# Layer 1 MLP of a two-layer diffusion backbone: places of a three-place weight ring, order of token sums at the seam, and the place of one transfer in POOL's queue

## The chip, the core and the metric

One core of one Trainium2 chip runs the whole program in one launch. Its engines are PE (TensorE, matmuls), DVE (VectorE), ACT (ScalarE), POOL (GpSimd) and SP (SyncE, which here only issues transfers). Each runs its own queue in order, and semaphores order them against each other. The metric is device microseconds of one execution.

## The reference

Two layers, each a token mixer and a squared-ReLU MLP, with D = 1024, 1024 latent tokens, 256 context tokens and a hidden width of 4096. Layer 0 mixes by a grouped Fourier transform, layer 1 by windowed attention; layer 1 updates the latent tokens alone. The part of the change is the MLP of layer 1:

```python
def _sq_relu_mlp(h, w1, w2):
    return jnp.square(jax.nn.relu(h @ w1)) @ w2
...
h_lat = h_lat + g2 * _sq_relu_mlp(_modulate(_rms_norm(h_lat, norm2_g[i]), sh2, sc2), mlp_w1[i], mlp_w2[i])
```

All is float32. Each product is made of three matmuls on rounded numbers: high times high, high times low, low times high. So each operand needs a rounded high half, which ACT writes, and a low half (the full number less the high one), which DVE or POOL writes.

## The kernel before

**The MLP of layer 1** is `strassen_tail` (from L1665). It takes the 4096 hidden rows in 16 pairs of 2 x 128. Pairs 0 and 1 (`PLAIN = 2`) compute the first product in the plain way, in four blocks for the hidden row block (1 or 2) and the token half. From pair 2 on both products go by Strassen's scheme with seven products, M1 to M7. The first-weight operands of a pair are items 0 to 6 (`W1_ORDER`), the token operands are B11, B21, B22 and the sums T1 to T4, which are made once, at the seam between pair 1 and pair 2, and then held.

**TensorE's order in a pair p** is M1, product 1 of pair p - 1, M5, product 2, M6, product 3, M2, product 4, M7, product 5, M3, product 6, M4, and then product 0 of pair p itself (`Z_ORDER`, `DEFERRED`, `pair` in the tensor block). Each is 12 matmuls of 128x128 by 128x512: M1 to M7 at L2763 to L2765, the second products in four groups of three at L2780 to L2782. Before group m of product i, TensorE waits until the result of group m of product i - 1 is read out of its bank (`read_out`): by DVE (`acc`, L2559) for m = 0, 1, 2, by ACT (`side_read`, L2247) for m = 3, which POOL then adds (`add`, L2082).

**The first weights' ring.** Item i of a pair lies in place i % 3 of `w1h` and `w1l`. For each item ACT rounds (`high1`, L2194) and POOL writes the low half (`low1`, L58 with `l_w1l`). `high1` waits for the product that last read the place: items 3 to 6 for M1, M5, M6, M2 of the same pair (`Z_ORDER[i - 3]`), items 0, 1, 2 for M4, M7, M3 of the pair before. In the queues of ACT and POOL, item 1 of the next pair comes first, then item 0, then item 2 (`HIGH1`). SP loads the full numbers into four slots (`load1`, `W1_SLOT`), each load behind the `low1` or the sum that last read the slot. Two items are sums that POOL makes in place (`sum1`, L2070).

ACT's queue of a pair (`pair` in the scalar block) is written out by hand, as are those of DVE and POOL. In it `high1(p, 6)` stands directly ahead of `relu(p, "B11")`. On DVE the order is `zsum(p, "B11")`, `acc(p - 1, 4, (0,))`, `square(p, "B11")`, `acc(p - 1, 4, (1, 2, 3))`. `square` reads what `relu` (L2223) wrote. M1 of a pair also waits for `relu` of B21 of the pair before, which ACT does behind M4.

**The seam.** The sums T1 to T4 are made on DVE in four operations each: `third_sum` (L2469), `first_sum` (L2475), `second_sum` (L2481), `fourth_sum` (L2487), each of which needs the one before. ACT rounds them (`high_t`, L2254), POOL writes the low half of T2, DVE those of T1, T3 and T4 (`low_t`). They are interleaved by hand with the work of pair 1. M5 of pair 2 needs T1 with its low half.

**The end of layer 0's MLP.** `layer_tail` also prepares sums of layer 1's weights in memory: per pair SP copies, and POOL issues two accumulating transfers (`add_sums`, L910, 512 KB each). The first weights' stands in the middle of `outputs`, the second weights' at its end. In the last pair the second is POOL's last instruction before all engines meet at the end of the block; then a block of one instruction clears the semaphores, and the attention's part begins. Layer 1's MLP waits for all these transfers before it loads its weights.

Of the kernel before, what the change touches and what calls it, by code (L numbers as in the profile page):

```python
# [562 lines left out]
def layer_tail(nc, sem, sb, banks, layer, wp, early, s_pw, w1, w2, mod, meanw, eps, ident, nh, nl, ht,  # L563
# [76 lines left out]
    with ExitStack() as ph:  # L640
# [124 lines left out]
        with nc.Block() as block:  # L765
# [94 lines left out]
            def _(pool):  # L860
# [51 lines left out]
                def outputs(p, more):  # L912
                    add(p, "M5")
                    low2(p, "S2")
                    add(p, "M3")
                    if more and C:
                        low1(p + 1, 0)
                    low2(p, "S3")
                    for prod in ROWS[2:]:
                        add(p, prod)  # L920
                        if C and not more:
                            if prod == "M2":
                                next_modulation()
                            for k in {"M6": (1,), "M7": (2, 3), "M4": (4,)}.get(prod, ()):
                                own_sum(k)
                        if prod == "M1":
                            for name in W_LATE[2:]:
                                low2(p, name)
                            if more:
                                low1(p + 1, 1 if C else 0)  # L930
                            if C:
                                add_sums(p, 0)
                    if more and not C:
                        low1(p + 1, 1)
                    if C:
                        add_sums(p, 1)
# [728 lines left out]
def strassen_tail(nc, sem, sb, banks, wp, early, s_pw, w1, w2, sums, s_sums, mod, meanw, eps, ident, nh, nl, nl_at, ht, park, out):  # L1665
# [31 lines left out]
    RELUS = ["B11", "B22", "B12", "B21"]  # L1697
    HIGH1 = [1, 0, 2, 3, 4, 5, 6]
    W1_SLOT = [0, 1, 0, 2, 1, 2, 3]
# [39 lines left out]
    with ExitStack() as ph:  # L1739
# [122 lines left out]
        def w1_parts(p, i):  # L1862
            if is_plain(p) and i == 3:
                return (x[:, 3].rearrange("p (k n) -> p k n", k=HK) for x in (ah, al))
            return w1h[:, i % 3], w1l[:, i % 3]

        def w1_at(p, i):
            if is_plain(p):
                return PRE + 4 * p + i + 1
            return p * 7 + (PRE + 4 * PLAIN - 7 * PLAIN + HIGH1.index(i) + 1)  # L1870

# [84 lines left out]
        with nc.Block() as block:  # L1956
            @block.sync
            def _(sp):
# [62 lines left out]
                load2(1, 6, (1, 2))  # L2021
                load1(2, 4, None, (2, 2))
                load2(2, 3, (1, 3))

                def pair(p, more):
# [11 lines left out]
                    if more:  # L2037
                        load1(p + 1, 4, None, (p + 1, 2))
                        load2(p + 1, 3, (p, 3))
# [13 lines left out]
            def _(pool):  # L2053
# [36 lines left out]
                def pair(p, more):  # L2090
# [10 lines left out]
                    if more:  # L2101
                        low1(p + 1, 1)
                    add(p - 1, 5)
                    low2(p, 1)
                    add(p - 1, 6)
                    low2(p, 2)
                    if more:
                        low1(p + 1, 0)
                        sum1(p + 1, 2)
                    add(p, 0)  # L2110
# [45 lines left out]
                low2(1, 1)  # L2156
                low1(2, 1)
                low1(2, 0)
                sum1(2, 2)
                low2(1, 2)  # L2160
                for j in range(HK):
# [13 lines left out]
            def _(act):  # L2175
                def high1(p, i):
# [10 lines left out]
                    elif i >= 3:  # L2187
                        act.wait_ge(s_z, z_at(p, Z_ORDER[i - 3]))
                    elif type(p) is int and p == PLAIN:
                        act.wait_ge(s_z, z_at(1, ("B12", "B12", "B21")[i]))  # L2190
                    else:
                        act.wait_ge(s_z, z_at(p - 1, Z_ORDER[(6, 4, 5)[i]]))
                    hi, _ = w1_parts(p, i)
# [62 lines left out]
                def pair(p, more):  # L2256
# [17 lines left out]
                    if more:  # L2274
                        high1(p + 1, 1)
                    relu(p, "B22")
# [10 lines left out]
                    if more:  # L2287
                        high1(p + 1, 0)
                    high(p, "T3")
                    side_read(p, 0)  # L2290
                    high(p, "T4")
                    high2(p, 3)
                    if more:
                        high1(p + 1, 2)
                    high(p, "T1")

# [84 lines left out]
                high2(1, 1)  # L2381
                relu(1, "B12")
                high1(2, 1)
                high1(2, 0)
                relu(1, "B22")
                high2(1, 2)
                for j in range(HK):
                    high_t("T2", j)
                high(1, "T2")
                high(1, "T3")  # L2390
                for j in range(HK):
                    high_t("T4", j)
                relu(1, "B21")
# [41 lines left out]
            def _(dve):  # L2435
# [227 lines left out]
                acc(0, 6)  # L2663

                low2(1, 0)
                sum2(1, 1)
                square(1, "B11")
                low(1, "B11")
                for one in (third_sum, first_sum):
                    for j in range(HK):  # L2670
                        one(j)
                square(1, "B12")
                for j in range(HK):
                    second_sum(j)
                square(1, "B22")
                diffs(1)
                low(1, "T2")
                for j in range(HK):
                    fourth_sum(j)
                low(1, "T3")  # L2680
                acc(1, 0, (0, 1))
                diff(1, "T4")
                acc(1, 0, (2, 3))
                pair(PLAIN, True)
# [20 lines left out]
            def _(pe):  # L2705
# [35 lines left out]
                def hidden(p, prod):  # L2741
# [16 lines left out]
                    for j in range(HK):  # L2758
                        (wh, wl), (th, tl) = (w1h[:, i % 3, j], w1l[:, i % 3, j]), tokens(name, j)
                        dst = z_ps[Z_BANK[prod]][:]  # L2760
# [1005 lines left out]
```

## Time and profile before

| | us |
|---|---|
| median of three runs (2436.36 to 2440.77) | 2439.2 |
| the profiled execution | 2440.93 |
| its span, first to last instruction | 2439.4 |

| engine | busy us | share of the span |
|---|---|---|
| PE, matmuls | 2262.4 | 93% |
| DVE | 1763.2 | 72% |
| POOL | 1173.2 | 48% |
| ACT | 1160.8 | 48% |

The mean granted TensorE clock is 0.975 of full speed. In a row of the timeline stand the start in us from the span's start, the duration, the engine, the line, what it writes and reads, and in brackets how long the engine was idle before it and which operation ended that. The idle time counts from the recorded end of the matmul before, which lies beyond the moment at which the next could have started. A busy engine is no bound by itself: what counts is which wait ends last before TensorE can go on.

### The profile page before, as it was taken

Reading aid. Unit: us, or ns where it says so; the run is one execution under the profiler, and the core shown is the slowest. Engines: PE = TensorE matmul, PEld = TensorE weight load, DVE = VectorE, ACT = ScalarE, POOL = GpSimd, SP = SyncE. Lnnn points to the kernel's source line nnn. Section 1 sums busy time; section 2 is a strip of 40 time slices with the busy share of each in tenths; the row PEclk is TensorE's granted clock in tenths of the full one; section 3 lists DMA queues with packets and bytes.
Section 4 is the critical chain, followed back from the end, with each engine's and each line's share of the span. In section 5 each row is a group of like instructions: output and inputs, shape, how many; then the busy total and the mean of one; then the engine's idle time right before and its main releaser. Section 6 shows DMA issues by size and latency. Waiting matters only on the chain. (4 is left out here: it accounts for less than half of the span.)

```text
span 2439.4 us, 38342 instructions
## 1 busy us (share of the span) xinstructions
PE 2262.4 (93%) x11430; PEld 1872.2 (77%) x11430; DVE 1763.2 (72%) x2843; ACT 1160.8 (48%) x2133; POOL 1173.2 (48%) x970
## 2 busy tenths in 40 slices
PE   5989979999999999999699799888998999999998
PEld 3768868888888888888587677776776777777777
DVE  4653787777777777777674688871689787878787
ACT  5553443333333333333443588883345554545454
POOL 0003623433333444333646477665546666666664
PEclk9999999999999999999799899999998999999999
DMA  7434213444443345444312211105111212121212
GB/s 267 177 131 174 65 52 104 122 127 120 113 128 103 112 123 132 114 114 131 122 49 104 88 31 38 33 24 198 48 43 48 73 56 73 56 73 56 73 56 87
DMA packets 106150, 234.23 MB, mean 96 GB/s; under 512 B 9424, under 2 KB 18000, under 8 KB 102736
## 3 DMA queue, kind: packets, MB, share of 16 engines
q1 hardware_dynamic: 94432, 209.57, 26.3%
q0 software_dynamic: 8704, 16.78, 4.2%
q10 hardware_dynamic: 2928, 6.82, 0.8%
q8 instruction: 43, 0.70, 0.1%
q14 instruction: 43, 0.35, 0.1%
HBM read 216.35 MB, written 50.33 MB: 109 GB/s over the span
## 5 line engine op out<-in xcount | busy, mean ns | idle before, releaser
L877 POOL TENSOR_TENSOR ht<-ht,l_side 128x512 f32<-128x512 f32 x112 | 150.3, 1342 | 508.9 <-ACT l_side L1002 504.7
L51 PE MATMUL l_z_ps<-nh,l_w1h 128*128 128x512 f32 (+1 forms) x816 | 292.8, 359 | 6.5 <-POOL l_w1l L58 3.4
L53 PE MATMUL l_z_ps<-nh,l_w1l 128*128 128x512 f32 (+1 forms) x816 | 291.8, 358 | 0.0
L52 PE MATMUL l_z_ps<-nl,l_w1h 128*128 128x512 f32 (+1 forms) x800 | 285.7, 357 | 0.0
L1306 DVE SCALAR_TENSOR_TENSOR ht<-l_yy_ps,mod,ht 128x512 f32<-128x512 f32 x336 | 233.8, 743 | 10.9 <-PE l_yy_ps L1622 9.9
L2082 POOL TENSOR_TENSOR ht<-ht,l_side 128x512 f32<-128x512 f32 x112 | 150.7, 1346 | 99.3 <-ACT l_side L2247 99.3
L58 POOL TENSOR_TENSOR l_w1l<-early,l_w1h 128x512 fp32r<-128x512 f32 x104 | 138.6, 1340 | 114.8 <-ACT l_w1h L2194 114.7
L3503 POOL TENSOR_TENSOR sc<-sc,den 128x640 f32<-128x640 f32 (+1 forms) x128 | 149.5, 1200 | 89.8 <-DVE den L3585 89.8
L58 POOL TENSOR_TENSOR l_w2l<-l_w2f,l_w2h 128x512 fp32r<-128x512 f32 x128 | 168.7, 1323 | 40.2 <-ACT l_w2h L2204 35.4
L2780 PE MATMUL l_yy_ps<-l_ah,l_w2h 128*128 128x512 f32 x448 | 178.5, 399 | 6.8 <-DVE ht L2559 6.7
L1620 PE MATMUL l_yy_ps<-l_ah,l_w2h 128*128 128x512 f32 x448 | 178.5, 398 | 6.1 <-DVE ht L1306 6.1
L51 PEld LDWEIGHTS l_z_ps<-nh,l_w1h 128*128 128x128 f32 x816 | 154.9, 190 | 30.4 <-issue 4.0
L2782 PE MATMUL l_yy_ps<-l_ah,l_w2l 128*128 128x512 f32 x448 | 176.3, 394 | 0.0
L1621 PE MATMUL l_yy_ps<-l_al,l_w2h 128*128 128x512 f32 x448 | 176.0, 393 | 0.0
L1622 PE MATMUL l_yy_ps<-l_ah,l_w2l 128*128 128x512 f32 x448 | 175.8, 392 | 0.0
L2781 PE MATMUL l_yy_ps<-l_al,l_w2h 128*128 128x512 f32 x448 | 175.2, 391 | 0.0
L53 PEld LDWEIGHTS l_z_ps<-nh,l_w1l 128*128 128x128 f32 x816 | 154.9, 190 | 22.6
L58 DVE TENSOR_TENSOR l_al<-l_slot,l_ah 128x512 fp32r<-128x512 f32 x144 | 122.7, 852 | 63.6 <-ACT l_ah L995 34.2
L52 PEld LDWEIGHTS l_z_ps<-nl,l_w1h 128*128 128x128 f32 x800 | 151.9, 190 | 21.8 <-issue 0.5
L1002 ACT ACTIVATE l_side<-l_yy_ps,mod 128x512 f32<-128x512 f32 x112 | 76.8, 686 | 183.1 <-PE l_yy_ps L1622 183.1
L58 DVE TENSOR_TENSOR l_w2l<-l_w2f,l_w2h 128x512 fp32r<-128x512 f32 x112 | 107.4, 959 | 54.0 <-ACT l_w2h L2204 42.9
L2559 DVE SCALAR_TENSOR_TENSOR ht<-l_yy_ps,mod,ht 128x512 f32<-128x512 f32 x192 | 136.7, 741 | 5.3 <-PE l_yy_ps L2782 5.3
(339 smaller groups left out, 6495.5 us busy)
## 6 DMA issues: line engine op xcount, KB each, us to landing
l_aw<-ada SPq DMA_DIRECT2D x128, 256.0 KB, 2.9
maw<-ada SPq DMA_DIRECT2D x24, 1024.0 KB, 5.1
l_w1f<-w SPq DMA_DIRECT2D x32, 512.0 KB, 3.6
l_w2f<-w SPq DMA_DIRECT2D x32, 512.0 KB, 4.2
sums<-w SPq DMA_DIRECT2D x32, 512.0 KB, 5.1
sums<-w POOLq DMA_DIRECT2D x32, 512.0 KB, 8.3
early<-w SPq DMA_DIRECT2D x50, 256.0 KB, 2.7
l_w2f<-w SPq DMA_DIRECT2D x48, 256.0 KB, 2.7
```

The lines of the kernel that those rows point to most:

```text
L51: pe.matmul(out, lh, rh, start=first, stop=False)
L52: pe.matmul(out, lh, rl, start=False, stop=False)
L53: return pe.matmul(out, ll, rh, start=False, stop=last)
L58: return eng.tensor_tensor(lo, full, f32(hi), ALU.subtract)
L1306: dve.scalar_tensor_tensor(out=h, in0=y_ps[m][:], scalar=mod[:, layer, G2, c, 0:1], in1=h, op0=ALU.mult, op1=ALU.add).then_inc(s_acc, 1)
L1620: pe.matmul(y_ps[m][:], wh, a_h, start=first, stop=False, skip_group_check=not first)
L1621: pe.matmul(y_ps[m][:], wh, a_l, start=False, stop=False, skip_group_check=not first)
L1622: pe.matmul(y_ps[m][:], wl, a_h, start=False, stop=True, skip_group_check=not first).then_inc(s_y, 1)
L2082: pool.tensor_tensor(h, h, side[k % 2][:], ALU.add).then_inc(s_add, 1)
L2780: pe.matmul(y_ps[m][:], wh, a_h, start=start, stop=False, skip_group_check=not start)
L2781: pe.matmul(y_ps[m][:], wh, a_l, start=False, stop=False, skip_group_check=not start)
L2782: pe.matmul(y_ps[m][:], wl, a_h, start=False, stop=True, skip_group_check=not start).then_inc(s_y, 1)
```

## The change

It does four things.

1. The ring's places come from a table, `W1_RING = [0, 1, 2, 0, 1, 2, 1]`, and `W1_AFTER = [3, 6, 5, 0, 1, 2, 4]` names for each item the product that last read its place (an index into `Z_ORDER`; of the pair before for items 0 to 2). So item 0 follows M2, item 1 M4, item 2 M3 of the pair before, and item 6 follows M7 of its own pair.
2. The items are made in the order 0 to 6 (`HIGH1` is gone): in the queues of ACT and POOL item 0 takes item 1's place and item 1 item 0's. `sum1(p + 1, 2)` and `high1(p + 1, 2)` move by a step each, and `load1(p + 1, 4)` waits for `low1(p + 1, 1)` too.
3. At the seam `third_sum` moves ahead of pair 1's work on DVE, `first_sum`, `second_sum` and `fourth_sum` each move ahead as well, and ACT's roundings of T2 and T4 go ahead of relus and roundings of pair 1.
4. In the last pair of layer 0 the second accumulating transfer is issued directly behind the first.

```diff
@@ outputs (POOL, layer_tail)
                             if C:
                                 add_sums(p, 0)
+                                if not more:
+                                    add_sums(p, 1)
                     if more and not C:
                         low1(p + 1, 1)
-                    if C:
+                    if C and more:
                         add_sums(p, 1)
@@ strassen_tail
-    HIGH1 = [1, 0, 2, 3, 4, 5, 6]
+    W1_RING = [0, 1, 2, 0, 1, 2, 1]
+    W1_AFTER = [3, 6, 5, 0, 1, 2, 4]
@@ w1_parts, w1_at, hidden
-            return w1h[:, i % 3], w1l[:, i % 3]
+            return w1h[:, W1_RING[i]], w1l[:, W1_RING[i]]
-            return p * 7 + (PRE + 4 * PLAIN - 7 * PLAIN + HIGH1.index(i) + 1)
+            return p * 7 + (PRE + 4 * PLAIN - 7 * PLAIN + i + 1)
@@ SP, also for pair 2 before the loop
-                        load1(p + 1, 4, None, (p + 1, 2))
+                        load1(p + 1, 4, (p + 1, 1), (p + 1, 2))
@@ POOL, pair (the same for pair 2 before the loop)
                     add(p - 1, 4)
                     if more:
-                        low1(p + 1, 1)
+                        low1(p + 1, 0)
                     add(p - 1, 5)
                     low2(p, 1)
+                    if more:
+                        sum1(p + 1, 2)
                     add(p - 1, 6)
                     low2(p, 2)
                     if more:
-                        low1(p + 1, 0)
-                        sum1(p + 1, 2)
+                        low1(p + 1, 1)
                     add(p, 0)
@@ ACT, high1
                     elif i >= 3:
-                        act.wait_ge(s_z, z_at(p, Z_ORDER[i - 3]))
+                        act.wait_ge(s_z, z_at(p, Z_ORDER[W1_AFTER[i]]))
...
-                        act.wait_ge(s_z, z_at(p - 1, Z_ORDER[(6, 4, 5)[i]]))
+                        act.wait_ge(s_z, z_at(p - 1, Z_ORDER[W1_AFTER[i]]))
@@ ACT, pair
                     relu(p, "B11")
                     side_read(p - 1, 4)
                     if more:
-                        high1(p + 1, 1)
+                        high1(p + 1, 0)
...
                     square_last(p)
                     if more:
-                        high1(p + 1, 0)
+                        high1(p + 1, 1)
                     high(p, "T3")
                     side_read(p, 0)
                     high(p, "T4")
                     high2(p, 3)
+                    high(p, "T1")
                     if more:
                         high1(p + 1, 2)
-                    high(p, "T1")
@@ ACT, the seam
                 relu(1, "B12")
+                high1(2, 0)
                 high1(2, 1)
-                high1(2, 0)
+                for j in range(HK):
+                    high_t("T2", j)
                 relu(1, "B22")
                 high2(1, 2)
                 for j in range(HK):
-                    high_t("T2", j)
+                    high_t("T4", j)
                 high(1, "T2")
                 high(1, "T3")
-                for j in range(HK):
-                    high_t("T4", j)
                 relu(1, "B21")
@@ DVE, the seam
+                for j in range(HK):
+                    third_sum(j)
                 low2(1, 0)
                 sum2(1, 1)
                 square(1, "B11")
                 low(1, "B11")
-                for one in (third_sum, first_sum):
+                for one in (first_sum, second_sum):
                     for j in range(HK):
                         one(j)
                 square(1, "B12")
                 for j in range(HK):
-                    second_sum(j)
+                    fourth_sum(j)
                 square(1, "B22")
                 diffs(1)
                 low(1, "T2")
-                for j in range(HK):
-                    fourth_sum(j)
                 low(1, "T3")
-                acc(1, 0, (0, 1))
                 diff(1, "T4")
-                acc(1, 0, (2, 3))
+                acc(1, 0)
```

## Rows read from the trace of the kernel before

**Rows 1.** Waits of TensorE from 1780 us on: waiter, awaited, us, times, longest.
```profile
PE l_z_ps L2763 <- POOL l_w1l L58: 19.2, 13, 2.7
```

**Rows 2.** Timeline: M1 of pairs 4 and 5, and ACT ahead of the latter.
```profile
1924.82 0.49 PE L2763 MATMUL l_z_ps<-nh,l_w1h 128*128 128x512 f32 x1 [1.38 <-POOL l_w1l L58]
1961.85 0.59 ACT L2223 ACTIVATE l_slot<-l_z_ps 128x512 f32<-128x512 f32 x1
1963.01 0.61 ACT L2194 ACTIVATE l_w1h<-early 128x512 fp32r<-128x512 f32 x1
1965.11 0.49 PE L2763 MATMUL l_z_ps<-nh,l_w1h 128*128 128x512 f32 x1 [1.37 <-POOL l_w1l L58]
```

**Rows 3.** Timeline around M7 of pair 4, and two roundings in a row at the seam.
```profile
1816.35 1.14 ACT L2194 ACTIVATE l_w1h<-early 128x512 fp32r<-128x512 f32 x2
...
1945.28 0.60 ACT L2223 ACTIVATE l_slot<-l_z_ps 128x512 f32<-128x512 f32 x1 [0.20 <-DVE l_z_ps L2518]
1945.91 0.70 DVE L2525 SCALAR_TENSOR_TENSOR l_z_ps<-l_z_ps,l_slot 128x512 f32<-128x512 f32 x1
1946.52 1.40 DVE L2559 SCALAR_TENSOR_TENSOR ht<-l_yy_ps,l_gneg,ht 128x512 f32<-128x512 f32 x2
1949.76 0.39 PE L2780 MATMUL l_yy_ps<-l_ah,l_w2h 128*128 128x512 f32 x1
1949.96 0.63 ACT L2194 ACTIVATE l_w1h<-early 128x512 fp32r<-128x512 f32 x1 [2.05 <-PE l_z_ps L2765]
```

**Rows 4.** Timeline: a read-out on DVE and the group that waited for it.
```profile
1791.81 2.05 DVE L2559 SCALAR_TENSOR_TENSOR ht<-l_yy_ps,l_gneg,ht 128x512 f32<-128x512 f32 x3
1792.60 0.50 PE L2780 MATMUL l_yy_ps<-l_ah,l_w2h 128*128 128x512 f32 x1 [1.29 <-DVE ht L2559]
```

**Rows 5.** Holes and clock: timeline rows, and stretches (A:B, us, busy, granted PEclk, DMA).
```profile
48.08 0.50 PE L51 MATMUL seq_ps<-tabh,gh 128*128 128x512 f32 x1 [1.73 <-ACT uvf L289]
48.00:51.00 3.00, 2.92 (x13) 2.38 (x14) 2.30 (x4) 2.48 (x6) 0.00 (x0) 1.00 0.87 350
1762.83 0.50 PE L51 MATMUL l_z_ps<-nh,l_ah 128*128 128x512 f32 x1 [2.00 <-POOL l_al L58]
1763.00:1766.00 3.00, 3.00 (x9) 2.33 (x10) 2.84 (x4) 0.94 (x2) 0.00 (x0) 0.56 0.30 87
1883.08 0.79 PE L2763 MATMUL l_z_ps<-nh,l_w1h 128*128 128x512 f32 x1 [2.67 <-POOL l_w1l L58]
1887.39 0.40 PE L2780 MATMUL l_yy_ps<-l_ah,l_w2h 128*128 128x512 f32 x1
```

**Rows 6.** Timeline of the seam: DVE, ACT, and M1 and M5 of pair 2.
```profile
1812.92 3.79 DVE L2469 SCALAR_TENSOR_TENSOR l_t3f<-l_nf,l_dsh,l_t3f 128x512 f32<-128x512 f32 x4
1819.64 6.29 DVE L2481 SCALAR_TENSOR_TENSOR l_t2f<-l_t3f,mod,l_t2f 128x512 f32<-128x512 f32 x4
1834.60 0.58 ACT L2223 ACTIVATE l_slot<-l_z_ps 128x512 f32<-128x512 f32 x1
1835.32 0.76 PE L2763 MATMUL l_z_ps<-nh,l_w1h 128*128 128x512 f32 x1 [5.63 <-ACT l_slot L2223]
1839.61 5.87 DVE L58 TENSOR_TENSOR nl<-l_nf,nh 128x512 fp32r<-128x512 f32 x4
1845.63 0.77 PE L2763 MATMUL l_z_ps<-nh,l_w1h 128*128 128x512 f32 x1 [3.09 <-DVE nl L58]
```

**Rows 7.** Line L2469: duration ns min/median/max, starts, forms.
```profile
L2469 DVE SCALAR_TENSOR_TENSOR l_t3f<-l_nf,l_dsh,l_t3f x4: 739/742/1798, 1812.9 to 1816.0; 128x512 f32<-128x512 f32 x4
```

**Rows 8.** Layer 0's end: the last two transfers' issues, and the drains (ns, start).
```profile
1176.14 1.05 POOL L910 DMA_DIRECT2D sums<-w  x1
...
1186.88 1.17 POOL L910 DMA_DIRECT2D sums<-w  x1
L765 POOLq DRAIN  x1: 8092/8092/8092, 1184.7 to 1184.7; - x1
L765 DVEq DRAIN  x1: 1554/1554/1554, 1186.0 to 1186.0; - x1
```

More of the change, by code:

```diff
@@ L2021, in _ @@
                 load2(1, 6, (1, 2))
-                load1(2, 4, None, (2, 2))
+                load1(2, 4, (2, 1), (2, 2))
                 load2(2, 3, (1, 3))
@@ L2156, in _ @@
                 low2(1, 1)
-                low1(2, 1)
                 low1(2, 0)
                 sum1(2, 2)
+                low1(2, 1)
                 low2(1, 2)
@@ L2758, in hidden @@
                     for j in range(HK):
-                        (wh, wl), (th, tl) = (w1h[:, i % 3, j], w1l[:, i % 3, j]), tokens(name, j)
+                        (wh, wl), (th, tl) = (w1h[:, W1_RING[i], j], w1l[:, W1_RING[i], j]), tokens(name, j)
                         dst = z_ps[Z_BANK[prod]][:]
```

## The prediction

> **What bounds the kernel now.** I read the waits of TensorE from 1780 us on first: the layer 1 MLP loop waits 13 times, 19.2 us in all, for POOL to write the low halves of a first weight [rows 1]. Then TensorE's timeline: the wait stands at M1 of each pair, 1.37 to 1.38 us of idle time twelve times over, and is 2.67 us once, at pair 3 [rows 2, 5]. Elsewhere in a pair TensorE issues back to back: from M1 of pair 4 to M1 of pair 5 are 40.29 us for 168 matmuls [rows 2]. Idle is counted from the recorded end of a matmul (0.40 us) though the next could start after 0.23, so each wait loses 1.37 + 0.17 = 1.54 us, and the first matmul behind it is drawn out (0.49 against 0.39), 0.10 more. That leaves 38.65 us, 0.230 for each matmul, and nothing else idle. So inside the loop TensorE bounds, with one hole per pair. Before the loop stand two larger holes, 5.63 us at M1 and 3.09 us at M5 of pair 2 [rows 6], and at the end of layer 0's MLP all engines wait for POOL [rows 8].
>
> **The hole at M1 goes.** Item 0 shared place 0 with item 6, so its rounding on ACT had to follow M4. In the rows: ACT relu of M4 at 1961.85, square, high1 at 1963.01, POOL's low1 behind it, M1 at 1965.11 [rows 2]. Now item 0 waits only for M2 of the pair before, which is four products earlier, and high1 and low1 for it stand right behind the side work of product 4. What is late next is `relu` of B21, done at 1961.85 + 0.59 = 1962.44, against 1963.57 for an unstalled M1: 1.1 us to spare. Item 1, now last behind M4, is wanted by M5, 5.5 us later, and takes over item 0's old slots on both engines. Saved: 12 x 1.64 = 19.7 us (pairs 4 to 15).
>
> **A new hole behind M7.** Item 6 now shares place 1 with item 4, so `W1_AFTER[6]` is 4 and `high1(p, 6)` waits for M7 instead of M2. Its place in ACT's queue is unchanged: just ahead of `relu(p, "B11")`. Behind that relu DVE's `square(p, "B11")` waits, and behind it on DVE the read-outs of product 4, which product 5 needs before it can reuse each bank. Now: relu 1945.28, square 1945.91, read-outs from 1946.52 [rows 3], while product 5 starts at 1949.76, so some 3 us to spare. After: count from the start P of product 5 (the end of M7). ACT notices M7 0.20 later (1949.96 against 1949.76); high1 to the next ACT instruction 0.52 (two such roundings in a row take 1.14, one 0.62); relu to square 0.63; square to read-out 0.61 [rows 3]; and TensorE starts 0.79 after the read-out starts (1791.81 to 1792.60) [rows 4]. Together P + 2.75. Group 0 of product 5 runs at P, group 1 could start at P + 0.69. Hole: 2.06, with the drawn-out first matmul 2.17. Group 2's read-out is 0.67 behind and just keeps up. 13 x 2.17 = +28.2 us (pairs 3 to 15). From both sides: if each hand-over took 0.05 less, 1.95, if one POOL operation or DVE contention came between, 2.4. DVE lags by 0.14 afterwards, less than the room at M1.
>
> **Queues passed.** On SP `load1(p + 1, 6)` waits for `low1(p, 6)`, now one product pair (5.5 us) later; its data is wanted a pair later, and the only load queued behind it waits for `low2(p, 2)` near the end of the pair anyway. `load1(p + 1, 4)` now waits for `low1(p + 1, 1)` as well, which ends where `low1(p + 1, 0)` ended before, and `sum1(p + 1, 2)`, one operation behind that until now, goes ahead of it: the load starts 1 to 2 us earlier. On POOL `low1(p, 6)` holds `add(p - 1, 4)` back by 5.5 us; that buffer is read into again only two products later. All nothing.
>
> **Pair 2.** It loses its M1-of-pair-3 hole: 2.67 + 0.17 idle, and the 12 matmuls take 4.31 us (1883.08 to 1887.39) instead of 2.76 [rows 5], 4.4 in all. It gains the hole behind M7, 2.17; and since four token sums (3.7 us) follow those read-outs on DVE there, I work out 0.7 and 0.7 us more at product 6, 0.7 at M1 and 0.4 in pair 3. Net +0.3 (-1.5 to +2).
>
> **The seam.** `third_sum` x4 (3.79 us) moves from behind `low(1, "B11")` [rows 6] to DVE's idle time before it, where only `low2` and `sum2` follow, due near 1810. So the other sums start 3.7 earlier, but run more beside POOL. An SBUF-only sum takes 0.74 us alone and 1.80 beside a POOL operation [rows 7]; the second sums took 6.29 [rows 6]. The Trainium skill (SBUF — State Buffer, Who interferes with whom) says that such a DVE instruction and a POOL instruction that reads SBUF block each other outright; the two durations agree, and by it the reordered sums pay again for each POOL operation beside them. Laid out with 0.74 for a free sum and 1.80 for one beside a POOL operation: first sums end at 1816.4 (one blocked), second at 1821.1, square of B12, fourth sums at 1827.3 (two low parts and the rounding of T2's on POOL between), square of B22 at 1827.3, differences and `low(T2)` to 1830.6. But the fourth sums no longer stand between `low(T2)` and `low(T3)`, and on ACT no longer ahead of `relu(1, "B21")`, which moves from 1834.60 to 1830.4. M1 starts at 1831.2 instead of 1835.32. Then `low(T3)` 31.9, T4, three read-outs to 34.5, `low(T4)` 35.5, the low parts of T1 (5.87 before, 5.3 here) to 40.7: M5 starts at 1840.8 instead of 1845.63. -4.8 us. The ends: these low parts beside an idle POOL, 4 x 0.7, -7.3; fourth sums wholly contended, -3.3. What is late next is the same low part of T1.
>
> **Layer 0.** The last accumulating transfer is issued by POOL at 1186.88, behind everything; POOL's drain then lasts from 1184.7 for 8.09 us, to 1192.8, and the other engines' last drain ends at 1186.0 + 1.55 = 1187.5 [rows 8]. The first one is issued at 1176.14. Issued right behind it, the second takes about 1 us of POOL's queue there, most of it taken up by POOL's later waits for ACT, so I let the sums and DVE end 0.3 later, at 1187.8 (an estimate). It then has 10 us to land before the engines meet, against the 6 us between issue and drain's end now. 1192.8 - 1187.8 = -4.9 us, rounded down. Bounds: 0, if the drain outlasts the other engines by as much as before for another reason; -5.3 (1192.8 less 1187.5) at most. I take the value near the second end, since the drain is long only where the issue stands right before it. Who waits for the transfer itself stands 500 us later.
>
> **Sum.** -4.9 - 4.8 + 0.3 - 19.7 + 28.2 = -0.9 us. The profiled execution took 2440.9 (span 2439.4), so 2440.0; the median is 2439.2, so **2438.3 us**. A measurement of this kernel tells 0.2%, 4.9 us, from no change.
>
> **Rivals.** *The clock falls in the new hole* (slower). The granted clock was 0.56 in 1763 to 1766, right behind 2.00 us of idle time, and full in 48 to 51, behind 1.73 [rows 5]; behind the twelve idle times of 1.37 the pace is full too, and behind 2.67 it is halved [rows 2, 5]. So the engine went from 2.4 to 1.2 GHz after the longer two. The new hole shows as 2.06 - 0.17 = 1.9 us, between the two. Each fall costs 4.31 us less the 2.86 of a drawn-out warm block, 1.45. From 4 falls in 14 holes on the result is slower than 0.2%; with 5, about a third, it is 2445.5, with all 2458.6. Against it: each of twelve holes of 1.37 left the clock alone, and 1.9 is less than any that did not. Chance 0.24. The Trainium skill (TensorE: Matmul & The Clock Gate, What's actually happening) says that the gate's timing is not tied to the kernel, so that equal stretches can come out differently; by it some of 14 equal holes would bring a fall and others not; no row here shows that.
> *The seam's sums run nearly free of POOL* and the hand-overs are at their short end: -2.5 and -1.6, 2434. Chance 0.12. For it: the end of one chain decides, and each contended step that falls away is worth 1.1.
> *No new hole*, since B11's chain had some slack that I misread: -0.9 - 28.2 - 2.2 and the follow-up stalls of pair 2, about 2405. Against it stands the order of ACT's queue in the code. Chance 0.05.
> *Layer 0's end does not move*, as the transfer holds POOL's drain or code and barrier take the time: 2443.2. Chance 0.09.
> The forecast keeps 0.50. Its own range is 2434 to 2443. The wanted 8 in 10 need the clock's middle case and the other seam end: 2432 to 2449. Faster by over 0.2% needs under 2434.3: the 0.05, most of the 0.12 and 0.03 of the forecast's edge, 0.19. Slower needs over 2444.1: 0.22 of the clock's, 0.04 of edges, 0.26. Same: 0.55.
>
> **What would show it.** In the profile after: no wait of M1 for POOL `l_w1l`; instead a wait of product 5's second matmul group (the lines that are L2780 to L2782 now) for DVE `ht`, 1.9 us, in every pair; ACT's low-numbered `l_w1h` rounding directly ahead of the B11 relu in time; a period of 38.65 + 2.17 = 40.8 us instead of 40.29; M1 of pair 2 1.5 us behind product 0's end, M5 3.5 us later; POOL's drain ending near 1187.8. The forecast is wrong if the period is under 40 (no hole), over 41.5 (clock falls or more than one hole), or if the stretch between the layers keeps its 4.9 us.

## The result and the profile after

The changed kernel takes 2445.86 us (median of 11 executions, 2439.54 to 2448.19) where the kernel before takes 2440.11 beside it: ratio 1.0023, 95% interval 1.0013 to 1.0032. It is slightly slower, not level. On another chip the same two kernels gave 2442.43 and 2440.70, ratio 1.0011 (1.0002 to 1.0021). The profiled execution of the changed kernel took 2440.84 us with a span of 2439.3, the same as the one before; that this is luck is shown further down.

The waits of TensorE from 1775 us on in the changed kernel (waiter, awaited, us in total, times, longest):

```profile
PE l_yy_ps L2783 <- DVE ht L2563: 34.6, 25, 2.9
PE l_z_ps L2766 <- DVE nl L58: 4.5, 1, 4.5
PE l_z_ps L2766 <- ACT l_slot L2227: 1.9, 2, 1.8
PE l_z_ps L2803 <- issue: 0.4, 1, 0.4
```

The wait of [rows 1] is gone. In its place product 5 waits for the read-outs of product 4. The timeline of the changed kernel around M7 of pair 4 (start, us, engine, line, operation, idle before and what ended it), which answers [rows 3]:

```profile
1940.00 0.63 ACT L2198 ACTIVATE l_w1h<-early 128x512 fp32r<-128x512 f32 x1 [6.99 <-PE l_z_ps L2768]
1940.54 0.58 ACT L2227 ACTIVATE l_slot<-l_z_ps 128x512 f32<-128x512 f32 x1
1941.15 0.70 DVE L2529 SCALAR_TENSOR_TENSOR l_z_ps<-l_z_ps,l_slot 128x512 f32<-128x512 f32 x1 [5.12 <-ACT l_slot L2227]
1941.76 1.40 DVE L2563 SCALAR_TENSOR_TENSOR ht<-l_yy_ps,l_gneg,ht 128x512 f32<-128x512 f32 x2
1942.55 0.50 PE L2783 MATMUL l_yy_ps<-l_ah,l_w2h 128*128 128x512 f32 x1 [1.90 <-DVE ht L2563]
...
1983.42 0.50 PE L2783 MATMUL l_yy_ps<-l_ah,l_w2h 128*128 128x512 f32 x1 [1.90 <-DVE ht L2563]
```

ACT rounds item 6 directly behind M7 (after 6.99 us with nothing to do, the wait of `W1_AFTER[6]`), then comes the relu of B11 0.54 later, `square` 0.61 later, the read-out 0.61 later, and TensorE 0.79 after that. The hole shows as 1.90 us idle and the next one stands 40.87 later. There is no other idle time in the pair.

The clock in one of these holes, of pair 13 of the same kernel. First the timeline, then two stretches (A:B, us, busy and count of PE, PEld, DVE, ACT, POOL, then the granted TensorE clock, the DMA share and GB/s):

```profile
2309.95 0.79 PE L2783 MATMUL l_yy_ps<-l_ah,l_w2h 128*128 128x512 f32 x1 [1.90 <-DVE ht L2563]
2310.54 0.63 PE L2784 MATMUL l_yy_ps<-l_al,l_w2h 128*128 128x512 f32 x1
```

```profile
2269.00:2271.00 2.00, 1.87 (x8) 1.52 (x9) 1.99 (x4) 0.60 (x1) 2.00 (x2) 1.00 0.35 131
2311.50:2313.50 2.00, 2.00 (x7) 1.58 (x6) 1.99 (x4) 0.30 (x1) 0.35 (x1) 0.53 0.08 31
```

Behind the hole of pair 12 (2269.1) the clock stays full. Behind that of pair 13, just as long, it is granted by half (1.2 instead of 2.4 GHz), and the matmuls take 0.63 instead of 0.39, until some 3.4 us later.

The seam and pair 2, on the timeline of the changed kernel, which answers [rows 6]:

```profile
1814.42 4.81 DVE L2491 SCALAR_TENSOR_TENSOR l_nf<-l_nf,mod,l_t2f 128x512 f32<-128x512 f32 x4
1822.33 0.59 ACT L2227 ACTIVATE l_slot<-l_z_ps 128x512 f32<-128x512 f32 x1
1823.07 0.47 PE L2766 MATMUL l_z_ps<-nh,l_w1h 128*128 128x512 f32 x1 [1.79 <-ACT l_slot L2227]
1827.37 5.85 DVE L58 TENSOR_TENSOR nl<-l_nf,nh 128x512 fp32r<-128x512 f32 x4
1827.58 1.74 POOL L58 TENSOR_TENSOR l_w2l<-l_w2f,l_w2h 128x512 fp32r<-128x512 f32 x1
1833.37 0.77 PE L2766 MATMUL l_z_ps<-nh,l_w1h 128*128 128x512 f32 x1 [4.54 <-DVE nl L58]
1858.03 0.51 PE L2783 MATMUL l_yy_ps<-l_ah,l_w2h 128*128 128x512 f32 x1 [1.90 <-DVE ht L2563]
1873.20 0.50 PE L2766 MATMUL l_z_ps<-nh,l_w1h 128*128 128x512 f32 x1 [0.16 <-ACT l_slot L2227]
1878.22 0.50 PE L2783 MATMUL l_yy_ps<-l_ah,l_w2h 128*128 128x512 f32 x1 [0.29 <-DVE ht L2563]
```

The hole ahead of M1 shrank from 5.63 to 1.79, that ahead of M5 grew from 3.09 to 4.54.

The end of layer 0, on the changed kernel's timeline, and its drains (ns, start), which answer [rows 8]:

```profile
1176.57 2.25 POOL L910 DMA_DIRECT2D sums<-w  x2
1187.01 1.26 POOL L883 TENSOR_TENSOR sqs<-sqs 128x512 f32<-128x512 f32 x1
1190.02 0.56 POOL L3036 MEMSET vs<- 128x256 f32 x2 [1.75 <-POOLq L76]
```

```profile
L765 POOLq DRAIN  x1: 3189/3189/3189, 1185.4 to 1185.4; - x1
L765 DVEq DRAIN  x1: 1106/1106/1106, 1187.8 to 1187.8; - x1
```

POOL's drain ends at 1188.6 instead of 1192.8, and DVE's, at 1188.9, is now the last.

### The profile page after: what moved, and what is told of

Its sections match the earlier page's. It is cut to its first block and busy times, and to the rows that moved or that the text cites. A ratio compares the mean times of both kernels' runs of the same rounds, so it can differ in the third digit from the quotient of the medians.

```text
span 2439.3 us, 38356 instructions
## 1 busy us (share of the span) xinstructions
PE 2259.3 (93%) x11430; PEld 1867.8 (77%) x11430; DVE 1772.6 (73%) x2843; ACT 1154.1 (47%) x2133; POOL 1180.1 (48%) x970
## 5 line engine op out<-in xcount | busy, mean ns | idle before, releaser
L877 POOL TENSOR_TENSOR ht<-ht,l_side 128x512 f32<-128x512 f32 x112 | 152.0, 1357 | 508.0 <-ACT l_side L1004 503.8
L2085 POOL TENSOR_TENSOR ht<-ht,l_side 128x512 f32<-128x512 f32 x112 | 157.8, 1409 | 56.5 <-ACT l_side L2251 56.5
L58 DVE TENSOR_TENSOR ptl<-t_ps,pth 128x512 fp32r<-128x512 f32 x152 | 105.0, 691 | 42.4 <-ACT pth L3547 39.2
```

The source lines that it names most:

```text
L58: return eng.tensor_tensor(lo, full, f32(hi), ALU.subtract)
```

## The experiments

All leave the computation whole. The theory was that of the prediction, completed by what the first profile showed: the hole behind M7 is a chain of hand-overs (ACT rounding, relu, square, read-out) that costs some 2.1 us in each pair, and on top of it the clock falls in some of these holes, 1.5 us each. The rivals: the hole has another cause (POOL or a bank) and stays when the rounding moves; the clock plays no part, and the loss comes from the seam or from contention.

**The changed kernel again, and ACT's order in it.** The first run is the changed kernel as it is. The second moves one line on ACT:

```diff
-                    high1(p, 6)
                     relu(p, "B11")
                     side_read(p - 1, 4)
+                    high1(p, 6)
                     if more:
                         high1(p + 1, 0)
```

> The changed kernel again, for a second profile. In the first one the period of a pair is 40.82 us, every pair has one hole of 1.90 us idle time behind M7, and the clock falls behind one of the 14; that execution took 2440.8 us where the median is 2445.9. Theory C (clock): the median execution has 4 to 5 falls where the profiled one had 1, each 1.45 us, so this profile's time less 1.45 for each fall in a hole behind M7 is 2439.4 within 1.5, whatever its time. Rival E (elsewhere): the median is longer by something outside the loop; the number of falls is 1 again also where the time is 2446, and the same subtraction gives 2444 or more.

> The changed kernel, but in ACT's queue the rounding of item 6 stands behind the B11 relu and the side work of product 4, ahead of item 0's. Both theories expect the hole behind M7 gone in all pairs and a period of 38.6 to 38.9 us. Theory C: with the holes the falls in them go as well: 14 x 2.17 = 30.4 and 2 us of follow-up waits in pair 2 less than the changed kernel without falls (2439.4), so 2407 us (2404 to 2411). Rival E: the excess of the median stays: 2445.9 - 32.4 = 2413.5. Rival H (the hole has another releaser, such as the low half on POOL): the hole stays, 2440 to 2446.

Unchanged: 2442.43 us (2439.45 to 2446.37), its profiled execution 2446.14. Neither expectation was met: that execution has 3 falls in the 14 holes, not 4 to 5 and not 1, and 2446.14 - 3 x 1.45 = 2441.8 lies between the two. So the falls are part of the excess, and something outside the loop is another part (it is taken up at the end of the next section). With item 6 rounded behind the relu and the side read: 2416.31 (2414.46 to 2419.68), ratio to the kernel before 0.9909 (0.9894 to 0.9924). The hole behind M7 is gone from every pair, and no fall of the clock is left in the loop. So ACT's in-order queue was the cause, and the rival with another releaser (2440 to 2446) is out. The time is above both other expectations (2407 and 2413.5), since a period of 38.6 to 38.9 was expected and it is 39.19. What came next is small, 0.25 us idle at the third group of product 1. The timeline of this kernel shows where it comes from:

```profile
1939.42 1.01 DVE L58 TENSOR_TENSOR l_w2l<-l_w2f,l_w2h 128x512 fp32r<-128x512 f32 x1 [0.39 <-ACT l_w2h L2208]
1939.83 1.75 POOL L2085 TENSOR_TENSOR ht<-ht,l_side 128x512 f32<-128x512 f32 x1
1940.47 1.67 DVE L2515 TENSOR_TENSOR l_w2f<-l_w2f 128x512 f32<-128x512 f32 x1
...
1953.55 0.50 PE L2783 MATMUL l_yy_ps<-l_ah,l_w2h 128*128 128x512 f32 x1 [0.25 <-DVE ht L2563]
```

POOL's add now falls on two DVE operations that touch SBUF alone, and `sum2` takes 1.67 instead of the 0.69 that it takes in the changed kernel; DVE is late from there on. The period is 39.19, between the 38.65 of a pair without holes and the 40.8 of the changed kernel.

**The length of the hole, both ways.** On DVE, more or fewer read-outs of product 4 ahead of `square`:

```diff
-                    acc(p - 1, 4, (0,))
+                    acc(p - 1, 4, (0, 1))
                     square(p, "B11")
-                    acc(p - 1, 4, (1, 2, 3))
+                    acc(p - 1, 4, (2, 3))
```

and in the other kernel `square(p, "B11")` ahead of all of DVE's.

> The changed kernel, but on DVE the read-outs of groups 0 and 1 of product 4 stand ahead of the square of B11 (before: group 0 alone). The hole moves from group 1 to group 2 of product 5 and shrinks from 2.06 to 1.37 us (1.2 us idle in a row), one size less than the 1.54 of the kernel before, at which its clock never fell. Theory C: no falls, 2439.4 - 14 x 0.69 = 2429.7 us (2427 to 2432), 16 less than the changed kernel's median. Rival E: only the 9.7 us go: 2436.2 us.

> The changed kernel, but on DVE no read-out of product 4 stands ahead of the square of B11. The hole moves to group 0 of product 5 and grows from 2.06 to 2.75 us. Without falls 2439.4 + 14 x 0.69 = 2449.1 us. Theory C: falls in more of the 14 holes than the 4 to 5 of the changed kernel, say 7 to 14: 2459 to 2469 us. Rival E: 2445.9 + 9.7 = 2455.5 us, whatever the number of falls.

Two ahead: 2432.11 us (2429.79 to 2437.45), ratio 0.9966 (0.9956 to 0.9976). None ahead: 2465.91 (2460.21 to 2468.44), ratio 1.0102 (1.0086 to 1.0117). The holes on the two timelines, of two read-outs ahead first:

```profile
1949.08 0.50 PE L2783 MATMUL l_yy_ps<-l_ah,l_w2h 128*128 128x512 f32 x1 [1.21 <-DVE ht L2563]
```

```profile
1949.64 0.49 PE L2782 MATMUL l_yy_ps<-l_ah,l_w2h 128*128 128x512 f32 x1 [2.76 <-DVE ht L2563]
1949.97 0.40 PE L2783 MATMUL l_yy_ps<-l_al,l_w2h 128*128 128x512 f32 x1
...
1951.11 0.63 PE L2784 MATMUL l_yy_ps<-l_ah,l_w2l 128*128 128x512 f32 x1
```

The hole moves one read-out to either side, from 1.90 to 1.21 and to 2.76 (2.59 in pair 2). Shortened by 0.69 in 14 pairs, it should give 9.7 us; it gave 2442.43 - 2432.11 = 10.3. That alone doesn't part the two theories: 2432.11 is just above the 2427 to 2432 of theory C, and 10.3 is far less than the 16 us that it counted from the median of 2445.9. The trace does: in none of the 14 holes of 1.21 (1.27 the last) did the clock fall, and from M1 of pair 4 to that of pair 15 are 441.4 us, 11 x 40.13. In pair 2 TensorE waits 1.05 us ahead of product 6.

Lengthened by 0.86 it should cost 12.0, and it cost 23.5. Behind 7 of the 14 long holes the clock fell; a pair takes 41.6 us without a fall, 43.3 with one, and 44.46 once, where the clock stayed low twice as long. By stretches, this execution against the mean of the four of the changed kernel (below): +17.1 from M1 of pair 4 to M1 of pair 15, of which 9.0 are the holes and 8 the clock, +2.4 behind that, +0.7 in pairs 2 and 3, and +3.2 ahead of M5 of pair 2, where the two kernels don't differ. So a hole has two prices, its own time and the clock's, and the second was higher for the longer hole.

**The three parts alone**, each on the kernel before: the ring with its order of items, the seam, and layer 0's transfer (the parts of the diff above).

> The kernel before with the ring's change alone (table of places, order of items, where the loop's items stand); seam and layer 0 as before. Theory C (the hole moves and grows from 1.54 to 2.06 us in 14 pairs instead of 13, and the clock falls in some of them): 6 to 9 us more without falls, by the stretches of the first two profiles, and 1.5 us for each of 2 to 5 falls, so 2450 to 2456 us. Rival F (my forecast before the result, no falls): 2446 to 2449. Rival N (the ring is neutral and the excess comes from the other parts): 2440.5.

> The kernel before with the order of the token sums at the seam alone. Theory C: the two holes at M1 and M5 of pair 2 shrink together by the 3.7 us that the profile of the changed kernel shows, 2436.8 us (2434.5 to 2438.5). Rival S (the seam's gain hangs on the ring's change): within 1.5 us of 2440.5.

> The kernel before with the place of the last transfer alone. Theory C: the meeting of the engines comes 3.9 to 4.3 us earlier and nothing behind it gives that back, 2436.4 us (2434.5 to 2438). Rival G (given back later, in the attention's part, whose length differed by 3 us between profiles): 2438.5 to 2440.5.

| kernel | us | ratio to the kernel before (2438.70) |
|---|---|---|
| ring alone | 2454.45 (2449.39 to 2454.55) | 1.0064 (1.0051 to 1.0076) |
| seam alone | 2436.75 (2435.20 to 2439.73) | 0.9993 (0.9985 to 1.0002) |
| layer 0 alone | 2435.15 (2430.31 to 2437.94) | 0.9983 (0.9975 to 0.9992) |

The ring loses, the transfer gains 3.6 us, and the seam's gain can't be told from nothing, although its stretch is 3.6 us shorter in the trace. The timeline of the seam alone shows that 2.2 us of that were given back in pair 2:

```profile
1838.07 0.77 PE L2762 MATMUL l_z_ps<-nh,l_w1h 128*128 128x512 f32 x1 [4.55 <-DVE nl L58]
...
1877.67 0.69 PE L2762 MATMUL l_z_ps<-nh,l_w1h 128*128 128x512 f32 x1 [3.13 <-POOL l_w1l L58]
```

From M5 of pair 2 to M1 of pair 3 are 39.60 us instead of 37.45. M1 of pair 3 waits 3.13 for POOL instead of 2.67 [rows 5], an idle time of 0.33 appears in product 6, and most of the rest is the clock behind M5's hole (4.55 instead of 3.09), which stayed low for 6.8 us instead of 3.4. The time of the seam alone is as theory C had it (2436.8), but the expectations took the kernel before as 2440.5 and it ran at 2438.70 beside these, so that the time alone doesn't shut out rival S. Layer 0 alone is within theory C's 2434.5 to 2438, and its ratio is clear of 1; rival G is out.

The ring alone is 13.3 us longer than the kernel before in the first profiled execution of each: 0.4 up to M5 of pair 2, 2.9 from there to M1 of pair 4, 7.8 to M1 of pair 15 and 2.3 behind it. Those are the new holes and the falls behind them; only pair 2 and the start of pair 3 have further idle times, 0.32 and 0.40 in product 6 and 0.52 at M1, which matter below.

The differences of the medians make +15.75 - 1.95 - 3.55 = +10.3, where the whole change gave +5.8 and +1.7. Under 2 us of the gap are pair 2: from M5 of pair 2 to M1 of pair 4 the seam costs 2.3 us on the kernel before and some 0.5 on the ring alone (means of 81.9 and 81.3). The rest may lie within what the executions of one kernel differ by (those of the kernel before ran from 2435.71 to 2442.15 beside these kernels), but that isn't shown.

**The order that removes the hole as well.** On ACT and POOL item 0 of the next pair goes first, where item 6 stood, and item 6 behind the side work of product 4 (not shown: the counts that follow the order, and the last pair):

```diff
@@ ACT, pair
-                    high1(p, 6)
-                    relu(p, "B11")
-                    side_read(p - 1, 4)
                     if more:
                         high1(p + 1, 0)
+                    relu(p, "B11")
+                    side_read(p - 1, 4)
+                    high1(p, 6)
@@ POOL, pair
-                    low1(p, 6)
-                    add(p - 1, 4)
                     if more:
                         low1(p + 1, 0)
+                    add(p - 1, 4)
+                    low1(p, 6)
```

> The changed kernel, but item 0 of the next pair takes item 6's old place in the queues of ACT and POOL (it waits for M2, as item 6 did before) and item 6 takes the one behind the side work of product 4. In the run with item 6 behind, a hole of 0.4 us was left per pair at product 1, and DVE's second sum took 1.67 us beside a POOL addition instead of 0.69. Theory P (that hole comes from POOL being late with its addition, since two low halves stood around it behind M7): with one low half each side the hole goes, period 38.7 us, 2410 us (2406 to 2413). Rival Q (the hole comes from DVE's own length once TensorE no longer waits anywhere): it stays, 39.1 us, 2414 to 2418.

2410.14 us (2408.72 to 2411.79), ratio 0.9888 (0.9874 to 0.9903): the fastest of all, 1.1% faster than the kernel before, 28.6 us. The period is 38.66 us, which is the 38.65 that the prediction worked out for a pair without any idle time, and the waits of TensorE from 1775 us on are down to this:

```profile
PE l_yy_ps L2790 <- DVE ht L2570: 7.3, 9, 2.9
PE l_z_ps L2773 <- DVE nl L58: 4.5, 1, 4.5
PE l_z_ps L2773 <- ACT l_slot L2234: 1.8, 1, 1.8
PE l_z_ps L2810 <- issue: 0.4, 1, 0.4
```

The 1.67 of `sum2` and the hole of 0.25 that it made are gone with it. The changed ring thus had all that was needed; one rounding stood in a place that had been free of waits as long as item 6 followed M2. Theory P had this time and this period; its rival, 2414 to 2418, is out.

**More profiled executions**, one each, to tie the time to the falls: the changed kernel twice more, the ring alone once more, and the kernel before once more.

> The changed kernel once more, unchanged, for one more profiled execution. Clock theory: the loop holds some 2 to 4 falls of the granted clock in its 14 new holes of 1.90 us, each worth about 1.5 us, so that pair 4 to the last pair takes 447.6 us plus 1.5 for each fall, and the whole execution 2438 to 2447 us, later with more falls. Rival, the clock plays no part in the loss: the stretch from M1 of pair 4 to that of pair 15 takes the same time whatever falls in it, and no fall is found in it.

> As the look before it: with the clock theory the time of the loop follows the number of falls in this execution at some 1.5 us each, on top of a floor that does not change; with the rival it does not.

> The ring's change alone once more, for a second profiled execution. It was 13 to 15 us slower than the kernel before where its holes alone are worth some 9 to 10. Clock theory: M1 of pair 4 to that of pair 15 takes 449.3 us plus about 1.5 for each fall of the granted clock in it, pair 3 takes 41.8 or, with a fall, 43.4, and the execution 2449 to 2455 us by their number. Rival, the ring alone costs more than the holes: a further idle time appears in each pair, or the stretches before pair 2 are longer than those of the kernel before.

> The kernel before, unchanged, for a second profiled execution. Clock theory: no fall of the granted clock in M1 of pair 4 to that of pair 15, which takes 443.1 us again within 0.3, 71.4 behind it; the stretches ahead of pair 2 (attention, projections, first product) differ from the first look by up to 5 us in all, since their longer holes bring a fall in one execution and not in another. Rival: the loop of the kernel before moves between executions as much as that of the changed one, and the comparison of the loops is luck.

They took 2444.46, 2442.94, 2452.66 and 2438.78 us. From the starts of TensorE's matmuls in the traces, with the falls in the holes (a fall is where the matmuls behind the hole go at 0.43 us apart instead of 0.23):

| execution | M1 of pair 3 to pair 4 | falls | M1 of pair 4 to pair 15 | falls | from there to the end |
|---|---|---|---|---|---|
| before, first | 41.74 | at M1 | 443.08 | 0 | 71.5 |
| before, second | 41.76 | at M1 | 443.24 | 0 | 71.5 |
| changed, first | 41.79 | 0 | 450.59 | 1 | 73.7 |
| changed, second | 43.34 | 1 | 451.03 | 1 | 73.7 |
| changed, third | 43.37 | 1 | 450.67 | 1 | 73.7 |
| changed, fourth | 41.81 | 0 | 449.24 | 0 | 73.7 |
| ring alone, first | 43.36 | 1 | 450.89 | 1 | 73.7 |
| ring alone, second | 43.35 | 1 | 451.06 | 1 | 73.7 |

Without a fall the eleven pairs take 449.24 = 11 x 40.84, with one they take 1.35 to 1.8 more; pair 3 takes 1.55 more. (The floor of 447.6 in my expectation was a slip; the period gives 449. And the two new executions of the changed kernel have 3 falls and 1, pair 2 counted, where 2 to 4 were expected.) The kernel before has no fall there and repeats within 0.2 us. So the rivals that the clock plays no part in the loop, and that the loop of the kernel before moves as much, are out. With pair 2 (a fall in all four executions of the changed kernel, in none of the ring alone) the six executions with holes of 1.90 us have 2, 3, 3, 1, 2 and 2 falls: 13 of 84 holes. They gather at the front: 4 of 6 in pair 2, 4 of 6 in pair 3, 5 of 72 in pairs 4 to 15. The ring alone's second execution shows no further idle time in the loop either, so that rival is out there, though not in pairs 2 and 3.

## Why the prediction was wrong

The means of the two executions of the kernel before and the four of the changed kernel, by stretch, against the forecast:

| stretch | before | changed | difference | forecast |
|---|---|---|---|---|
| start to the first matmul of the attention's part | 1193.2 | 1189.3 | -4.0 | -4.9 |
| to the first second product of pair 0 | 584.0 | 583.1 | -0.9 | 0 |
| to M5 of pair 2 | 67.2 | 63.7 | -3.5 | -4.8 |
| to M1 of pair 4 | 79.2 | 81.9 | +2.7 | +0.8 |
| to M1 of pair 15 | 443.2 | 450.4 | +7.2 | +5.8 |
| to the end | 71.5 | 73.7 | +2.2 | +2.2 |
| sum | | | +3.7 | -0.9 |

These are profiled executions; their +3.7 lies between the +5.8 and the +1.7 of the medians.

**The mechanism held.** M1's wait went, the new one came where the prediction had put it, with the length that it had worked out: 1.90 us of idle time, which with the 0.17 that the record hides is the 2.06 (to 0.01), and a period of 40.84 against 40.8. In the execution of the changed kernel without a fall from pair 3 on, the eleven pairs take 449.24 us against 443.16, +6.1, where the forecast's 2.17 - 1.64 = 0.53 for a pair makes +5.8, and the last pair, which has a new hole and no M1 behind it, takes +2.2 against +2.2. The rival without a hole (2405) is out, and the other order on ACT shows what it would have been worth.

**The step that failed is how the clock was taken into the sum.** The prediction had its price right, 1.45 us for a fall (1.35 to 1.8 measured), and had no fall in the likeliest case, because the holes of 1.37 and one of 1.73 had none and 1.90 was less than the shortest idle time seen with one, 2.00 [rows 5]. So it treated as a threshold what one hole on either side had shown, and gave the clock a chance as a whole instead of a term. The trace of the kernel before held a row against that, in the attention's part:

```profile
1638.97 0.47 PE L3654 MATMUL pv_ps<-pth,vw 128*128 128x512 f32 x1 [1.65 <-DVE ptl L58]
...
1640.93 0.79 PE L3654 MATMUL pv_ps<-pth,vw 128*128 128x512 f32 x1 [0.82 <-DVE ptl L58]
```

```profile
1640.60:1643.80 3.20, 2.87 (x9) 2.27 (x10) 1.10 (x3) 0.79 (x2) 3.14 (x5) 0.50 0.00 0
```

Behind idle times of 1.65 and 0.82, shortly after one another, the clock halved; in the second execution of the same kernel the same two idle times, 1.65 and 0.83, left it full (granted clock 1.00 from 1639.0 to 1642.5). What the runs showed behind M1 and M7 is a share: none of 48 holes of 1.37 to 1.39, 13 of 84 of 1.90, 7 of 14 of 2.76. Of the 4.6 us by which the table exceeds the forecast, some 2.5 are the clock's (1.1 here and 1.4 in pairs 2 and 3), the largest term. With 14 new holes even a share of one in six is 2 falls, so the likeliest case should have held +3 us. Over the forecast, the table has +1.4 behind M1 of pair 4, where 3 falls in 4 executions make 1.1, and +1.9 ahead of it, which the next point takes apart.

**Pairs 2 and 3 (+0.8 forecast from M5 of pair 2 to M1 of pair 4, +2.7 measured).** In the changed kernel the stalls at product 6 that I had worked out, 0.7 twice, don't show: M1 of pair 3 waits 0.16 to 0.20 and one group behind it 0.29. But in all four executions the clock fell in pair 2's new hole, and TensorE came to product 6 later by it. In the ring alone, where the pair's queues are the same and the clock didn't fall there, the stalls stand in both executions (the timeline of the first):

```profile
1869.49 0.50 PE L2782 MATMUL l_yy_ps<-l_ah,l_w2h 128*128 128x512 f32 x1 [1.90 <-DVE ht L2561]
...
1874.93 0.50 PE L2782 MATMUL l_yy_ps<-l_ah,l_w2h 128*128 128x512 f32 x1 [0.32 <-DVE ht L2561]
...
1876.29 0.50 PE L2782 MATMUL l_yy_ps<-l_ah,l_w2h 128*128 128x512 f32 x1 [0.40 <-DVE ht L2561]
...
1884.68 0.50 PE L2765 MATMUL l_z_ps<-nh,l_w1h 128*128 128x512 f32 x1 [0.52 <-ACT l_slot L2225]
```

With the 0.17 of each they are 0.49, 0.57 and 0.69 where the forecast had 0.7 three times. From M5 of pair 2 to M1 of pair 3 this execution takes 38.69 us, and the two of the changed kernel with the same clock behind M5 take 38.77 and 38.85: here the fall cost 0.1 net, not 1.45, since it hides the stalls. The +1.9 over the forecast is then, in the means: 0.5 for pair 3, which takes 41.8 without a fall and not 0.4 but 1.0 more than a later pair, 0.1 for this fall, 0.5 for the clock behind M5's hole (grown to 4.54 us, it brought a low clock of 6.8 us instead of 3.4 in two of four executions), and 0.8 for falls in pair 3 in two of four. No execution of the changed kernel is without the fall in pair 2, so this comparison goes across two kernels; the one with two read-outs ahead, which has the new seam and no fall there, waits at the same three places (1.05, 0.39 and 0.51). Of the time saved at M1, 1.45 us came back as idle time ahead of M5.

**The seam (-4.8 forecast, -3.5 measured, -3.7 in the first execution).** Counted from pair 0's second product, M1 came 0.4 later than worked out and M5 1.1. Half of that is one term, the low parts of T1: I let them shrink from 5.87 to 5.3, and they stayed at 5.85, since two POOL operations (1.74 and 1.71 us instead of 1.3) lie beside them. The Trainium skill (SBUF — State Buffer, Who interferes with whom) says that such DVE and POOL instructions shut each other out. These rows agree with it (5.85 us, and 1.74 and 1.71 on POOL), and `sum2` with its 1.67 us above does so too.

**Layer 0 (-4.9 forecast, -4.0 measured).** The drain of POOL shrank from 8.09 to 3.19 us, as expected (it ends 4.7 us after the issue at 1186.88 is over, and now 0.3 after POOL's last sum), so the rival that the end doesn't move (2443.2) is out. The estimate that failed is the price in POOL's own queue: two issues take 2.25 us where one took 1.05 [rows 8], and the waits for ACT took up only a small part. POOL's last sum ends at 1188.27 instead of 1186.93; 0.43 of that the execution was late already when the first transfer was issued (1176.57 against 1176.14), 0.9 is the second issue's, three times the 0.3 that I had allowed. DVE's drain behind it ends at 1188.9, where I had 1187.8.

**That the first two profiles agree is luck.** In the changed kernel's first execution the stretch from the attention's part to pair 0's second product, which the change doesn't touch, took 579.8 us; in the other three it took 585.2, 585.0 and 582.4, and before 584.5 and 583.5. The granted clock was low for 62 us of that stretch in the first, and for 72 to 75 us in the other five. That it was up to 5 us quick there hid the loss behind it. Read from single executions, this change is worth nothing; it takes the stretches one by one, or medians, to see the 2 to 6 us.

**The range** for eight in ten, 2432 to 2449, held the time, at its upper part; the forecast's own, 2434 to 2443, didn't. The chance of slower, 0.26, stood mostly on four or more falls, where fewer falls (1 to 3 in the profiled executions) and two mis-sized gains (1.3 and 0.9 us) were enough.

## What to carry to other kernels

When a wait is taken off one instruction by letting another operand share the place, look at what stands behind the newly waiting instruction in its in-order queue: here one rounding of 0.6 us held a relu, a square and three read-outs, two of them on DVE, and moving it two places turned a loss of 2 to 6 us into a gain of 24. A hole in TensorE's work has a second price, the clock behind it. Count it as a share of the holes by their length, not as a threshold, and rate a hole that is lengthened higher than the same time in short ones. The two prices don't always add: a fall can hide stalls that stand right behind it, so look for an execution without the fall before calling a stall absent.

## What the runs showed of the hardware

The granted clock doesn't fall in all holes of one length. Of 14 equal idle times of 1.90 us it fell in one, two or three by the execution; from pair 4 on, in the four executions of the changed kernel, it fell in pair 13, 12, 8 and nowhere. No idle time of about 1.8 ahead of M1 of pair 2 (nine executions) brought a fall. The Trainium skill (TensorE: Matmul & The Clock Gate, What's actually happening) says that the gate isn't in step with the kernel, so that equal stretches can come out unequal; these runs agree with it. Falls are more frequent at the front (8 of 12 in pairs 2 and 3, 5 of 72 later); why, wasn't tried.

With an accumulating transfer of 512 KB issued as POOL's last instruction, POOL's drain takes 8.09 us, and 3.19 with the transfer issued 10 us earlier; two issues in a row take 2.25 us of POOL's time where one takes 1.05.

A stretch that an edit doesn't touch can differ by 5 us in 584 between executions, and does so with the time at the low clock in it: 579.8 us with 62 us of it, 582.4 with 72, 585.2 with 75. The long loop of the kernel before, without falls, repeats within 0.2 us in 443.
